# Expert weights loaded as two experts by neighbouring rows, 8192 bytes a packet, instead of four experts by one row

## The reference, cut to what matters

```python
def expert_choice_ffn(h, w_router, w_gate, w_up, w_down):   # first block, each of 2 layers
    # 16 experts, each takes 32 tokens: x is [16, 32, 1024]
    # w_gate, w_up: [16, 1024, 1024]; w_down: [16, 1024, 1024]
    y = (silu(x @ w_gate) * (x @ w_up)) @ w_down            # then scattered back, weighted
...
def hier_moe(h, wg, bg, we, be, w_gate, w_up, w_down):      # second block, 1 layer
    # 4 groups of 8 experts = 32 experts, top 2 of the best group for each token
    # w_gate, w_up: [32, 1024, 512]; w_down: [32, 512, 1024]
```

## Time and profile before

| | |
|---|---|
| median of three runs | 2273.24 us (2272.0 to 2279.18) |
| profiled execution: span of the trace | 2272.4 us |
| the profile gives no own time beside the span; median less span | 0.84 us |
| TensorE busy, VectorE, ScalarE | 76%, 29%, 24% of the span |
| TensorE's granted clock, mean | 0.887 of full speed |
| DMA | 748.76 MB in 226975 packets, mean 330 GB/s |
| span of the expert stages on TensorE | 286 to 749, 1020 to 1509, 1797 to 2260 us |

### The profile page before, as it was taken

One profiled execution on the slowest core, in us unless ns is written; L12 is line 12 of the kernel. 1 busy time (PEld: TensorE's weight loads), 2 busy tenths in 40 slices (PEclk: granted clock), 3 DMA queues, 4 the chain that ended last, 5 costly groups with the idle time before them and its releaser, 6 DMA issues.

```text
span 2272.4 us, 29204 instructions
## 1 busy us (share of the span) xinstructions
PE 1719.1 (76%) x12802; PEld 1052.0 (46%) x12802; DVE 660.5 (29%) x1074; ACT 554.7 (24%) x849; POOL 0.2 (0%) x4
## 2 busy tenths in 40 slices
PE   7989976565565999997676766669999976667665
PEld 6978932020111897892222323238988722222221
DVE  3477510000000447750250111037557400000001
ACT  3456300000000336630101221033444311010101
POOL 0000000000000000000000000000000000000000
PEclk9999998888788999998889889889999987777877
DMA  9732899999999963389999999983424999999996
GB/s 362 265 120 97 309 408 409 409 409 410 409 409 408 356 238 117 124 307 408 410 406 402 406 404 406 409 313 112 149 93 165 399 408 410 410 410 410 410 410 265
DMA packets 226975, 748.76 MB, mean 330 GB/s; under 512 B 6064, under 2 KB 18608, under 8 KB 226224
## 3 DMA queue, kind: packets, MB, share of 16 engines
q1 hardware_dynamic: 226864, 747.11, 84.5%
HBM read 746.04 MB, written 1.05 MB: 329 GB/s over the span
## 4 chain that ended last, share of the span: by engine, by line
DMA 40%; PE 39%; SPq 11%; ACT 4%; DVE 4%; issue 2%; DVEq 0%; ACTq 0%
PE bank L716 18%; DMA ring<-w_expert_down 16%; SPq L2785 11%; DMA ring<-w_expert_up 10%; DMA ring<-w_expert_gate 6%; PE bank L719 5%; PE bank L773 4%; DMA arena<-moe_w_up 3%; PE bank L797 2%; DMA ring<-moe_w_up 2%; PE bank L950 1%; PE bank L807 1%; DMA ring<-moe_w_down 1%; PE bank L970 1%; DMA ring<-ada_w 1%
## 5 line engine op out<-in xcount | busy, mean ns | idle before, releaser
L773 PE MATMUL bank<-ring,arena 128*32 128x512 f32 x2560 | 392.6, 746 | 235.0 <-DMA ring<-w_expert_up 110.2
L797 PE MATMUL bank<-ring,arena 128*32 128x512 f32 x1280 | 213.5, 802 | 167.8 <-DMA ring<-w_expert_down 132.7
L716 PE MATMUL bank<-arena_parts,ring_parts 128*128 128x256 f32 x1376 | 313.6, 283 | 2.4 <-DVE ring_parts L2430 1.6
L773 PEld LDWEIGHTS bank<-ring,arena 128*32 128x32 f32 x2560 | 79.3, 124 | 505.6 <-issue 162.8
L716 PEld LDWEIGHTS bank<-arena_parts,ring_parts 128*128 128x128 f32 x1376 | 232.7, 189 | 11.5 <-issue 3.1
L1495 ACT ACTIVATE arena<-bank 128x512 f32<-128x512 f32 (+1 forms) x150 | 76.0, 535 | 521.7 <-PE bank L787 252.5
L797 PEld LDWEIGHTS bank<-ring,arena 128*32 128x32 f32 x1280 | 40.7, 131 | 323.9 <-DMA ring<-w_expert_down 193.1
L2012 DVE TENSOR_TENSOR arena<-arena,bank 128x512 f32<-128x512 f32 x24 | 15.8, 685 | 592.4 <-PE bank L773 592.4
L716 PE MATMUL bank<-ring_parts 128*128 128x256 f32 x768 | 151.2, 287 | 11.7 <-DVE ring_parts L2430 5.3
L716 PE MATMUL bank<-hnT_parts,ring_parts 128*128 128x256 f32 x544 | 154.0, 283 | 0.0
L716 PEld LDWEIGHTS bank<-ring_parts 128*128 128x128 f32 x768 | 123.7, 192 | 14.8 <-issue 5.2
(11 more groups left out here) (353 smaller groups left out, 2384.4 us busy)
## 6 DMA issues: line engine op xcount, KB each, us to landing
ring<-w_expert_down SPq DMA_DIRECT2D x64, 2048.0 KB, 23.9
ring<-w_expert_up SPq DMA_DIRECT2D x60, 2048.0 KB, 23.7
ring<-w_expert_gate SPq DMA_DIRECT2D x56, 2048.0 KB, 23.6
ring<-w_in SPq DMA_DIRECT2D x34, 2048.0 KB, 11.0
ring<-moe_w_up SPq DMA_DIRECT2D x24, 2048.0 KB, 23.8
ring<-moe_w_gate SPq DMA_DIRECT2D x20, 2048.0 KB, 23.7
ring<-moe_w_down SPq DMA_DIRECT2D x16, 2048.0 KB, 23.8
arena<-moe_w_down SPq DMA_DIRECT2D x16, 2048.0 KB, 23.5
```

Of the source, the lines that this page charges most:

```text
L716: last = pe.matmul(out[:, n * S:(n + 1) * S], w[:, k, n * P:(n + 1) * P], x[:, k, :], start=first, stop=final)
L773: last = pe.matmul(banks[bank0 + f][32 * e:32 * e + 32, :], x_slots[:, c, 32 * e:32 * e + 32], w[:, k, e, f * 512:(f + 1) * 512], start=c ...
L797: last = pe.matmul(banks[4 + d][32 * e:32 * e + 32, :], hidT[:, f, 32 * e:32 * e + 32], w[:, e, d * 512:(d + 1) * 512], start=f == 0, stop ...
```

## The change

A unit is still 2 MB and there are as many units as before. It now holds two experts of the tile instead of four, and for each of them two neighbouring rows a partition (first block and both down matrices) or four (gate and up of the second block), so that a partition gets two pieces of 8192 bytes instead of four of 4096. Units of experts 0 and 1 and units of experts 2 and 3 alternate. Partition p now holds rows 8p to 8p+7 everywhere (4p to 4p+3 for the second block's down), so a piece starts every 32 KB (gate, up and down of the first block), every 16 KB in the second block. To match, TensorE reads the gathered features and the hidden values with a step of 8 (or 4) floats in `tile_slots` and in the transposes, and the second block's `token_rows` copy on ScalarE writes its output in plain order. `TAKEN = 1`: TensorE waits for one unit at a time, and its eight matmuls go to the column groups of two experts only.

```diff
+UNIT_E = 2
+UNIT_GROUPS = TILE_E // UNIT_E
+TAKEN = 1
...
+        def unit_counts(f_width):
+            rows = UNIT // f_width // UNIT_E
+            return DC * UNIT_GROUPS // rows, f_width // P * UNIT_GROUPS * D * UNIT_E // UNIT
...
-                        last = pe.matmul(out[:, cols], hn[:, half, c * P:(c + 1) * P], pick_of(half),
-                                         start=half == 0, stop=half == TH - 1)
+                        rows = hn[:, half, :].rearrange("t (q c) -> t c q", c=DC)[:, c, :]
+                        last = pe.matmul(out[:, cols], rows, pick_of(half), start=half == 0, stop=half == TH - 1)
...
+                def part(u, per):
+                    e0 = (u % UNIT_GROUPS) * UNIT_E
+                    return u // UNIT_GROUPS * per, range(e0, e0 + UNIT_E)
...
                             for f in range(halves):
-                                for e in range(TILE_E):
-                                    last = pe.matmul(banks[bank0 + f][32 * e:32 * e + 32, :],
-                                                     x_slots[:, c, 32 * e:32 * e + 32],
-                                                     w[:, k, e, f * 512:(f + 1) * 512],
-                                                     start=c == 0, stop=c == DC - 1)
+                                for u in units:
+                                    w = place(u).rearrange("p (e k f) -> p k e f", k=in_rows, e=UNIT_E)
+                                    for i, e in enumerate(part(u - u0, in_rows)[1]):
+                                        last = pe.matmul(banks[bank0 + f][32 * e:32 * e + 32, :],
+                                                         x_slots[:, c, 32 * e:32 * e + 32],
+                                                         w[:, k, i, f * 512:(f + 1) * 512],
+                                                         start=c == 0, stop=c == DC - 1)
...
-                        last = pe.transpose(out[:, f * P:(f + 1) * P], hid[:, (4 * j + f) * P:(4 * j + f + 1) * P],
-                                            ident)
+                        cols = hid[:, 0:f_width].rearrange("p (q c) -> p c q", c=fc)[:, 4 * j + f, :]
+                        last = pe.transpose(out[:, f * P:(f + 1) * P], cols, ident)
...
-                place = hn_tok[:, half, :].rearrange("t (k c q) -> t c q k", k=DC, c=DC)[:, c0:c0 + 4]
-                act.activation(place, banks[4 + j][:].rearrange("t (c q k) -> t c q k", c=4, k=DC), ACT.Copy,
+                act.activation(hn_tok[:, half, c0 * P:(c0 + 4) * P], banks[4 + j][:], ACT.Copy,
...
+                n_in, n_out = unit_counts(f_width)
+                src = gate if u < n_in else up if u < 2 * n_in else down
+                n = u % n_in if u < 2 * n_in else u - 2 * n_in
+                e0 = t * TILE_E + n % UNIT_GROUPS * UNIT_E
+                cols = UNIT // UNIT_E
+                rows = src[bass.ds(e0, UNIT_E), :, :].rearrange("e (p r) x -> p e (r x)", p=P)
+                first = n // UNIT_GROUPS * cols
+                load(at, slot(at).rearrange("p (e x) -> p e x", e=UNIT_E), rows[:, :, first:first + cols], loaded)
```

More of the change, by code:

```diff
@@ L760, in expert_tile @@
                 for which, bank0 in (("gate", 4), ("up", 6)):
[L761 to L767, removed]
+                    u0 = n_in if which == "up" else 0
+                    for n in range(0, n_in, TAKEN):
+                        units = range(u0 + n, u0 + n + TAKEN)
+                        for u in units:
+                            loaded(u)
+                        c0, _ = part(n, in_rows)
+                        for k in range(in_rows):
+                            c = c0 + k
+                            if which == "gate" and n % UNIT_GROUPS == 0 and c % 2 == 0:
                                 if c in between:
@@ L771, in expert_tile @@
                             for f in range(halves):
-                                for e in range(TILE_E):
-                                    last = pe.matmul(banks[bank0 + f][32 * e:32 * e + 32, :],
-                                                     x_slots[:, c, 32 * e:32 * e + 32],
-                                                     w[:, k, e, f * 512:(f + 1) * 512],
-                                                     start=c == 0, stop=c == DC - 1)
-                        steps = [f"{name} unit {u}"] + ([f"{name} {which}"] if n == n_in - 1 else [])
-                        last.then_inc(pe_done, pe_p.mark(*steps))
-                        behind(u)
+                                for u in units:
+                                    w = place(u).rearrange("p (e k f) -> p k e f", k=in_rows, e=UNIT_E)
[4 more added lines that the diff above has]
+                                                         start=c == 0, stop=c == DC - 1)
+                        steps = [f"{name} unit {u}" for u in units]
+                        last.then_inc(pe_done, pe_p.mark(*steps, *([f"{name} {which}"] if n == n_in - TAKEN else [])))
+                        for u in units:
+                            behind(u)
                 if turn:
@@ L786, in expert_tile @@
                     for f in range(4):
-                        last = pe.transpose(out[:, f * P:(f + 1) * P], hid[:, (4 * j + f) * P:(4 * j + f + 1) * P],
-                                            ident)
+                        cols = hid[:, 0:f_width].rearrange("p (q c) -> p c q", c=fc)[:, 4 * j + f, :]
+                        last = pe.transpose(out[:, f * P:(f + 1) * P], cols, ident)
                     last.then_inc(pe_done, pe_p.mark(f"{name} hidT{j}"))
                 pe.wait_ge(act_done, act_at(f"{name} hidT{fc // 4 - 1}", loops))
[L791 to L801, removed]
+                for n in range(0, n_out, TAKEN):
+                    units = range(2 * n_in + n, 2 * n_in + n + TAKEN)
+                    for u in units:
+                        loaded(u)
+                    f0, _ = part(n, out_rows)
+                    for k in range(out_rows):
+                        f = f0 + k
+                        for d in range(2):
+                            for u in units:
+                                w = place(u).rearrange("p (e k d) -> p k e d", k=out_rows, e=UNIT_E)
+                                for i, e in enumerate(part(u - 2 * n_in, out_rows)[1]):
+                                    last = pe.matmul(banks[4 + d][32 * e:32 * e + 32, :], hidT[:, f, 32 * e:32 * e + 32],
+                                                     w[:, k, i, d * 512:(d + 1) * 512], start=f == 0, stop=f == fc - 1)
+                    steps = [f"{name} unit {u}" for u in units]
+                    last.then_inc(pe_done, pe_p.mark(*steps, *([f"{name} down"] if n == n_out - TAKEN else [])))
+                    for u in units:
+                        behind(u)
                 for j in range(4):
```

3 lines of the change are left out of this document (1 added, 2 removed).

## The result

The changed kernel takes **2259.1 us** (2258.93 to 2259.7, 4 runs) against 2273.88 for the kernel before (2272.0 to 2279.18, 4 runs): ratio 0.9929, 95% interval 0.9915 to 0.9944. That is 14.8 us faster where 33 were forecast. The time lies outside the forecast case's own range of 2230 to 2250; that the wider range of 2228 to 2282 holds it is luck, because that range was wide for the sake of rivals 1 and 3, and neither of them came true.

The account below looks back on a forecast made before the run. Expert stages were taken as bound by weight DMA, 5.12 us a unit. Terms -39.8 + 5.7 + 1.7 - 0.5 = -32.9 us gave 2240 us, with an 8-in-10 range of 2228 to 2282.

Parts of the forecast that it names:

- forecast case: Whole kernel: DMA stays the bound with units 4.97 us apart, giving 2240 us, own range 2230 to 2250; 54%.
- rival 1: Second block: TensorE becomes the bound through half-width units of 3.44 us plus strided loads; 2262 us (2250 to 2280); 20%.
- rival 3: Expert-stage DMA: 8192-byte packets bring nothing, units stay 5.12 us apart, only losses remain; 2280 us (2270 to 2290); 10%.
- Packets: Expert-stage weight DMA: 8192-byte packets give 422 GB/s, 4.97 us a unit, 0.15 us saved on 265 units, 39.8 us.
- rival 4: Expert-stage DMA: the two short windows are right, 4.83 us a unit, 77 us saved, 2203 us; 5%.
- Half-width unit: TensorE in expert stages: 3.44 us a unit at high clock (3.6 with drain), 1.72 more, mostly hidden under DMA's 4.97.
- Clock: TensorE in the expert stages: expected at the high level for nearly all of the stages, above 0.9.
- rival 2: TensorE in the stages: half-width units fail to hold the high clock, 6.8 us when slow; about 2390 to 2600 us; 9%.
- Strided operands: Gathers and transposes on TensorE: 32-byte steps counted as 0, from above 0.135 us a load, 39 us in second block.
- At the stage starts: First slots come free later: one 2 us hole per first-block layer and 1.7 in the second block, 5.7 us lost.
- Stage ends: Last unit of a stage is exposed: 1.7 us lost in layer 1, about unchanged in layer 0 and second block.
- The plain copy: Second block's ScalarE copy in token_rows becomes plain; about one of four stands ahead of the gather, 0.5 us gained.

Follow-up runs that it names:

- all start edits: Changed kernel plus unpermuted gather reads, two gate units run together in first-block first tiles and every other second-block tile, and later second-block gathers: 2238.78 us, ratio 0.9842.
- plain gathers: Changed kernel, but gathers read 128 neighbouring floats and ScalarE's copies write the features permuted in both blocks: 2248.84 us, ratio 0.9879.
- pairs at the first block's starts: Changed kernel, but gate units of each first-block layer's first tile run two together on four column groups: 2247.76 us, ratio 0.9882.
- both 18: Changed kernel with two-together gate units in the first block's first tiles and gathers reading neighbouring floats, second block's order unedited: 2241.02 us, ratio 0.9853.
- the pairs: Changed kernel with TAKEN = 2: TensorE waits everywhere for two units of the same rows and runs them together on four column groups: 2259.13 us, ratio 0.9924.

## Why the prediction was wrong, point by point

- **Packets: right.** 8192 bytes at 421 to 422 GB/s, units 4.97 to 4.99 us apart; 422 and 4.97 were forecast. The 39.8 us are there: all start edits shorten the stages by 36.5, with holes left over. Rivals 3 (5.12 us a unit) and 4 (4.83) fell with these 4.97. A packet of 8192 bytes takes 16 x 8192 / 421.5 = 311 ns and two of 4096 take 320, so one packet saves 9 ns. That is the 9.4 of the forecast and not the 3.5 that was worked out from the Trainium skill ("DMA: Bandwidth & Descriptors", "Why small descriptors are slow").
- **Half-width unit: right alone, wrong in company.** 3.63 us for a unit that stands alone (3.6 forecast). But a further landed one adds 1.75, not 3.0 to 3.44; the margin over whole tiles was wider than thought, and rival 1 lost its ground: the second block runs at DMA's rate.
- **Clock: right in the steady stretch, not at the starts.** 0.98 to 1.00 in the stages, so rival 2 fell. But the prediction priced the first units of a stage at the high clock, and units 0 and 1 of layers 0 and 1 took 4.3 and 5.32 us instead of 3.63.
- **Strided operands: size right, place wrong.** The gathers' loads in the changed kernel, whose line before stands in the earlier trace rows (ns min/median/max):

```profile
L752 PEld LDWEIGHTS bank<-arena x512: 312/335/340, 287.9 to 2199.2; 128*128 128x128 f32 x171
```

  335 ns against 192 is 0.143 us more, a little above the 0.135 that was taken from ScalarE as the upper bound. The Trainium skill's rule of a penalty for each other 16-byte line ("SBUF — State Buffer", "Door 1: The DMA port swizzle") agrees in sign, for a read by TensorE; that rival 1 comes true by it was too much, since that section gives no size. In the steady stretch that is hidden, as forecast: the second block runs at 422 GB/s. The error was to count it as zero at the stage starts, where 16 such loads stand ahead of unit 0 and 8 ahead of each of two later pairs. The experiment with plain gathers gets 10 us back, of which a part is the clock. (The slack of "some 58" us that the prediction works out for 3.0 us a unit is 59.8 by its own numbers; nothing hangs on it.)
- **"At the stage starts": the step that failed.** The prediction counted "one hole of 2 us in each layer of the first block and 1.7 in the second: 5.7 us", since "SP's later issues wait behind that one, and the units behind them have 20 us of queue by then". They measure 24.2. There is no queue at that moment: all slots ahead are landed or in flight, and DMA lives on what the next free slot gives it. The lag of the frees grows from one to the next, because between them stand a gather with strided loads, routing work, and a half-width unit that has no neighbour; what counts is the sum up to the worst of them (in layer 0 +3.0 us at the first, +9.1 at the third), less the slack. Before, that slack was just enough there (0.1 us of hole over 285 to 345 us), so the later delay was paid nearly in full, 8.8 us. In the second block the first free slot alone is 5.2 us later, since strided gathers, one more gather and half-width matmuls stand ahead of it. The prediction priced the first free slot, by half width alone and at the high clock, and stopped.
- **Stage ends: right.** The last unit of layer 1 takes 3.63 us at 1493.11, 1.92 before.
- **The plain copy: not seen.** From the last down unit of layer 1 to the second block's first gather, 14 traces lie between 291.3 and 294.0 us, with no order by the form of the copy; a term of 0.5 is below that scatter.

The sum goes wrong by one term: put 24.2 in the place of 5.7, and -32.9 becomes -14.4, against -14.8 measured. That it fits so closely is partly luck. The 2.3 us more that are lost in the middle of layer 1 aren't in it, and the windows are good to a us or two each. The lengths of the stages give another measure: 18.0 us less, where the forecast has 39.8 - 5.7 - 1.7 = 32.4, so they are 14.4 short. By that the losses that were priced at 5.7 are 20.1, the middle of layer 1 with them. The other 3 us of the difference in span lie outside the stages: the first gather of layer 0 comes 1.7 us later and the stretch ahead of the second block is 1.8 us longer, and both places scatter by as much over the other traces. So the failed term is some 18 to 24 us and not 5.7. The shares of its causes overlap: plain gathers alone give back 10 us, pairs at the first block's starts 11, both 18. All start edits are 2 us below both, but the intervals overlap, so what the second block's edits give isn't shown.

What stays open: what half width costs with 4096-byte packets; whether the pairs' loss in the middle of layer 1 is their waiting or the clock; and what the low clock at the starts costs in time of the whole. The timelines give it 2.4 us of the third issue's lag in layer 0 (it was 0.56 and 0.59 over 300 to 304 us), but the run with pairs in the first gates had 0.50 to 0.54 over 296 to 302 as well and lost much less. No run took the clock alone.

## What to carry to other kernels

Where a stream of transfers is the bound and its buffers are full when the consumer starts, list the times at which the first several buffers come free, not only the first, and hold each against the transfer time of a buffer: here the loss in layer 0 was close to the worst lag of the list and three times the first. A cost that is hidden in the steady stretch is paid in full there, so look for what can be moved out from between the first consumers, or do just those at full width. And when a change brings its steady gain but half the total, take windows of a few microseconds at every stage start before doubting the gain.

## What the runs showed of the hardware that was not expected

- Float32 matmuls on two of TensorE's four column groups overlap with those of the other two that come later in the program: blocks of 8 instructions fully (16 in 1.94 us), units of 16 by half (32 instructions end 1.75 us after 16 would). With routing work, a gather or a wait for a transfer in between, a unit stands alone and takes 3.63 us at the high clock.
- A TensorE weight load of 128 x 128 float32 from a source with a step of 32 bytes takes 335 ns, from neighbouring floats 192.
- Over 2000 to 2100 us, at the same 422 GB/s, the granted clock was 1.00 with half-width units (TensorE busy 86.7 us) and 0.85 with pairs on four column groups (71.7 us): at the mean of the second the engine was at its low level, 1.2 GHz, for part of the time.
